# Rotating the queries of the last layer on VectorE across row groups, two tiles at once, in place of rotation matmuls

## What is computed

```python
def rope(t, pos):
    half = MLA_ROPE // 2          # 32
    ...
    t1 = t[..., :half].astype(jnp.float32)
    t2 = t[..., half:].astype(jnp.float32)
    return jnp.concatenate([t1 * cos - t2 * sin, t1 * sin + t2 * cos], axis=-1).astype(t.dtype)

q = (rms_norm_2(c_q, mla_q_norm_w) @ mla_w_uq).reshape(b_, l_, MLA_HEADS, MLA_NOPE + MLA_ROPE)
kv = (rms_norm_2(c_kv, mla_kv_norm_w) @ mla_w_ukv).reshape(b_, l_, MLA_HEADS, MLA_NOPE + MLA_V)
q_nope, q_rope = q[..., :MLA_NOPE], rope(q[..., MLA_NOPE:], positions)
```

## Time and profile before

| | us |
|---|---|
| median of three runs | 1755.0 (1753.88 to 1757.76) |
| profiled execution, device time | 1759.86 |
| its span, first to last instruction | 1758.1 |
| TensorE busy in matmuls | 1714.0 (97%) |
| VectorE busy | 1304.2 (74%) |
| ScalarE busy | 906.0 (52%) |
| GpSimd busy | 182.9 (10%) |
| mean granted TensorE clock | 0.990 |

### The profile page before, as it was taken

The page is one execution under the profiler, slowest core; times in us unless marked ns, Lnnn a source line. Parts: engine busy times, 40 slices in busy tenths (PEclk is TensorE's granted clock), DMA queues, the critical chain, the costliest instruction groups (busy, mean ns, idle before and its releaser), DMA issues.

```text
span 1758.1 us, 24063 instructions
## 1 busy us (share of the span) xinstructions
PE 1714.0 (97%) x9505; PEld 1471.9 (84%) x9505; DVE 1304.2 (74%) x1616; ACT 906.0 (52%) x1178; POOL 182.9 (10%) x200
## 2 busy tenths in 40 slices
PE   6899999999999999999999999999999999999997
PEld 5778888887888888888888888888888888888886
DVE  6889979786787766887677788966566667778654
ACT  6344443444465445665454667644444445566543
POOL 4321101011010110111010010001111000000001
PEclk9989999999999999999999999999999999999999
DMA  9989979774455566666677555666666565444563
GB/s 356 384 285 339 351 227 318 231 255 149 144 168 169 191 181 189 183 190 204 182 217 211 158 166 170 183 191 192 188 191 180 168 195 147 138 132 132 168 190 109
DMA packets 312288, 357.00 MB, mean 203 GB/s; under 512 B 11633, under 2 KB 285169, under 8 KB 312177
## 3 DMA queue, kind: packets, MB, share of 16 engines
q1 hardware_dynamic: 295792, 296.24, 55.9%
q0 software_dynamic: 16384, 59.22, 9.7%
HBM read 353.29 MB, written 2.13 MB: 202 GB/s over the span
## 4 chain that ended last, share of the span: by engine, by line
PE 70%; DVE 16%; ACT 6%; issue 4%; DMA 2%; POOL 1%; SPq 0%; DVEq 0%; ACTq 0%
PE psG L491 40%; PE psG L492 20%; DVE w_lo L421 6%; ACT w_hi L417 3%; DMA raw<-in_mem_w 2%; PE psG L485 2%; PE psG L487 2%; PE psG L486 2%; DVE ada_sum L1327 1%; DVE P L1275 1%; PE psH L1943 1%; DVE P L1280 1%; PE psH L1926 1%; DVE W L1830 0%; DVE gate_sum L1327 0%
## 5 line engine op out<-in xcount | busy, mean ns | idle before, releaser
L491 PE MATMUL psG<-xA,w_hi 128*128 128x512 f32 x2624 | 945.8, 404 | 1.2 <-DVE w_lo L421 0.6
L421 DVE TENSOR_TENSOR w_lo<-raw,w_hi 128x1024 fp32r<-128x1024 f32 (+1 forms) x560 | 697.2, 1258 | 209.2 <-ACT w_hi L417 207.5
L492 PE MATMUL psG<-xA,w_lo 128*128 128x256 f32 x2624 | 737.6, 281 | 0.0
L417 ACT ACTIVATE w_hi<-raw 128x1024 fp32r<-128x1024 f32 (+1 forms) x560 | 569.0, 1042 | 224.0 <-PE psG L492 164.8
L491 PEld LDWEIGHTS psG<-xA,w_hi 128*128 128x128 f32 x2624 | 494.9, 189 | 120.8 <-issue 4.7
L492 PEld LDWEIGHTS psG<-xA,w_lo 128*128 128x128 f32 x2624 | 497.8, 190 | 2.3 <-issue 1.4
L491 PE MATMUL psG<-yP,w_hi 128*128 128x512 f32 x960 | 337.3, 397 | 2.2 <-DVE yP L1888 1.0
L492 PE MATMUL psG<-yP,w_lo 128*128 128x256 f32 x960 | 267.8, 279 | 0.0
L491 PEld LDWEIGHTS psG<-yP,w_hi 128*128 128x128 f32 x960 | 180.2, 188 | 46.1 <-DVE yP L1888 1.3
L460 ACT ACTIVATE P<-psG 128x512 f32<-128x512 f32 (+2 forms) x103 | 60.8, 590 | 238.1 <-PE psG L492 238.1
L492 PEld LDWEIGHTS psG<-yP,w_lo 128*128 128x128 f32 x960 | 180.8, 188 | 0.0
(11 more groups left out here) (345 smaller groups left out, 1772.3 us busy)
## 6 DMA issues: line engine op xcount, KB each, us to landing
raw<-in_w_in SPq DMA_DIRECT2D x360, 512.0 KB, 3.8
raw<-in_w_out SPq DMA_DIRECT2D x128, 512.0 KB, 3.5
ada_ring<-in_w_ada POOLq DMA_DIRECT2D x96, 512.0 KB, 6.3
raw<-in_mem_w SPq DMA_DIRECT2D x32, 512.0 KB, 10.2
raw<-in_w_uq SPq DMA_DIRECT2D x24, 384.0 KB, 3.4
raw<-in_w_ukv SPq DMA_DIRECT2D x32, 128.0 KB, 2.5
raw<-in_w_ukv SPq DMA_DIRECT2D x16, 256.0 KB, 3.4
P<-in_memT SPq DMA_DIRECT2D x4, 512.0 KB, 7.2
```

The source lines that it names most:

```text
L417: nc.scalar.activation(high(n), low(n, raw), ACT.Copy).then_inc(hi_ready, 1)
L421: nc.vector.tensor_tensor(low(n), low(n, raw), high(n), ALU.subtract).then_inc(lo_ready, 1)
L491: nc.tensor.matmul(psG[:, bank + f, :], hi[:, w], x, start=first, stop=False)
L492: last = nc.tensor.matmul(psG[:, bank + f, S:2 * S], lo[:, w], x[:, 0:S], start=False, stop=end)
```

## The change

VectorE does the whole rotation, and does it for the two tiles of a unit together at place 3 of the G_UK half; place 3 of the G_UV half is empty. The product with cos goes over both tiles (128 rows, 512 columns). For the product with sin four instructions of 32 rows and 512 columns each read one group of 32 rows and write the neighbouring one. The sign that the rotation matrix carried is put into the table of sin once, in unit 0, by two instructions on rows 32 to 63 and 96 to 127. TensorE's rotation matmuls and the semaphore `rq_rot` are gone; `rq_done` counts to 4.

```diff
             def rope_hook(u, bb, p):
...
-                if p == 3:
-                    r = 2 * u + bb
-                    x = P[:, QT + 3 * r + 2, :]
-                    landed(dve, G_UQ, (3 * r + 2) // 2 + 1)
-                    dve.wait_ge(q["rq_rot"], r + 1)
-                    v.tensor_tensor(t_cos, x, cos, ALU.mult)
-                    link(v.tensor_tensor(t_sin, psH[:, BA, 0:S], sin, ALU.mult))
-                    v.tensor_tensor(x, t_cos, t_sin, ALU.add).then_inc(q["rq_done"], 1)
+                if bb == 0 and p == 3:
+                    if u == 0:
+                        for row in (32, 96):
+                            ins = v.tensor_scalar(sin[row:row + 32], sin[row:row + 32], -1.0, None, ALU.mult)
+                        link(ins)
+                    x = P[:, QT + 6 * u + 2:QT + 6 * u + 6:3, :]
+                    landed(dve, G_UQ, 3 * u + 3)
+                    v.tensor_tensor(x_cos, x, cos2, ALU.mult)
+                    for row in (0, 32, 64, 96):
+                        to, of = slice(row, row + 32), slice(row ^ 32, (row ^ 32) + 32)
+                        ins = v.tensor_tensor(x_sin[to], x[of], sin2[of], ALU.mult)
+                    link(ins)
+                    v.tensor_tensor(x, x_cos, x_sin, ALU.add).then_inc(q["rq_done"], 1)
...
-                if p == 2:
-                    r = 2 * u + bb
-                    if r:
-                        pe.wait_ge(q["rq_done"], r)
-                    else:
-                        pe.wait_ge(q["rk_done"], 1)
-                    landed(pe, G_UQ, (3 * r + 2) // 2 + 1)
-                    mm(psH[:, BA, 0:S], C("rot64"), P[:, QT + 3 * r + 2, :], start=True, stop=True)\
-                        .then_inc(q["rq_rot"], 1)
```

More of the change, by code:

```diff
@@ L241, in build @@
             "ma_s ma_mx ma_p ma_pn ma_t ma_pt ma_o ma_y sc_cv sc_tap sc_done f2_y f2_hi f2_lo "
-            "rp_red rp_tab rk_rot rk_done rq_rot rq_done cn_sq cn_pre cn_ss cn_rs cn_h cn_hi cn_lo "
+            "rp_red rp_tab rk_rot rk_done rq_done cn_sq cn_pre cn_ss cn_rs cn_h cn_hi cn_lo "
             "ml_s ml_mx ml_p ml_pn ml_t ml_pt ml_o ml_y zc_done m3_y m3_hi m3_lo f3_y f3_hi f3_lo fin_y gained last"
@@ L1789, in _ @@
             t_cos, t_sin = P[:, ROPE_T, :], P[:, ROPE_T + 1, :]
+            x_cos, x_sin = P[:, ROPE_T:ROPE_T + 2, :], P[:, ROPE_T + 2:ROPE_T + 4, :]
+            cos2, sin2 = (x.unsqueeze(1).broadcast_to([NP, 2, S]) for x in (cos, sin))
             dve.wait_ge(q["rp_tab"], 1)
@@ L1814, in _ @@
             dve.wait_ge(loaded["late"], 32)
-            dve.wait_ge(q["rq_done"], 8)
+            dve.wait_ge(q["rq_done"], 4)
             v.tensor_copy(W[64:128, 0:S], P[64:128, KR, :])
@@ L2192, in _ @@
                     run_products(pe, g, ukv_hook)
-            pe.wait_ge(q["rq_done"], 8)
+            pe.wait_ge(q["rq_done"], 4)
             pe.wait_ge(q["rk_done"], 2)
```

## The result

The changed kernel took 1772.5 us (median of 4 runs, 1769.0 to 1775.0), before 1755.7 alongside; ratio 1.0086, 95% interval 1.0066 to 1.0106. It is slower, by 16.8 us. The forecast was 1771.7 us, +16.7.

A forecast was written before the change was run, and what follows sets the result against it. VectorE's rotation of each unit's first tile, ahead of L1672 for which TensorE's L1926 waits, was taken to bound the stage. Order +11.1 and clock +5.6 gave +16.7 us: 1771.7 us against the median 1755.0, range 1763.5 to 1777.

The forecast's parts named there:

- TensorE has no slack at the turn: TensorE's turn of the probabilities (L1926) waits for VectorE's scaling (L1672); its idle time grows from 0.15 to 3.7 us.
- Short instructions cost like full ones: Each 32x512 product with sin on VectorE costs like a full 128x512, 688 ns; group 4.21 us in place of 1.13.
- Rival B: 32-row instructions on VectorE are cheap: group 2.16 us, +2.9 us in all, 1758 us, no change; chance 0.05.
- Changing rows costs the overlap: VectorE instructions on other rows than the one ahead do not overlap: 0.72 us per step in place of 0.60.
- Rival C: Moves between row groups on VectorE are slower, 0.5 us more per sin product: 8 us more, near 1780 us; chance 0.07.
- Eight rotation matmuls are worth 1.7 us, not 3.4: On TensorE only the four removed in the G_UV halves gain, 0.43 us each; those in the G_UK halves only lengthen waiting.
- Two sign flips +0.75 us, tail -0.3 us: VectorE's two sign flips in unit 0 add 0.75 us; without the last rotation, L1676 after unit 3 comes 0.3 us earlier.
- Order alone +11.1 us: Stage cost without the clock: 4 x (3.08 - 0.43) + 0.75 - 0.3 = +11.1 us.
- The fall of the clock +5.6 us: TensorE's clock falls from 2.4 to 1.2 GHz after each unit's wait: 1.4 us per unit, +5.6 us over four.
- two such stretches: Two four-microsecond stretches of slow TensorE clock, perhaps in one unit; a bound only, each stretch priced at 1.7 us.
- rival A: TensorE's clock stays at 1.00 through the waits: +9.0 to +11.1 us, 1764 to 1766 us; chance 0.28.
- the forecast's span: Kernel time with the fallen clock: 1768 us (overlapping price) to 1776 us (stalls at 1.7, unit 0 twice); chance 0.60.

The follow-up runs named there:

- e3: Changed kernel with the rotation behind the scaling of the probabilities on VectorE, not ahead of it: stage 58.3 us, kernel 1757.2 us, ratio 1.0003.
- e4: Kernel before, with its own one-tile rotation moved behind the scaling of the probabilities: stage 59.5 us, kernel 1755.9 us, ratio 0.9998.
- e2: Changed kernel with one 128x512 product with sin in place of the four of 32 rows, leaving out the swap of halves: stage 61.9 us.
- e7: Changed kernel rotating by rows, but one tile in each half of a unit, six instructions over 256 columns each time: stage 69.2 us.
- e8: Changed kernel with all four short products reading and writing rows 0 to 31, rotation not computed: group 3.72 us, stage 77.7 us.
- e6: Changed kernel with two tiles at a time, but rotated by one TensorE matmul per unit and one product with sin: stage 61.2 us.
- e5: e3 with VectorE's keys' tile preparation right behind the last rotation and TensorE's last-copy wait moved later: stage 56.0 us, kernel 1752.6 us, ratio 0.9977.
- e1: Changed kernel with 14 throwaway matmuls per unit filling TensorE's wait for the scaled probabilities: stage 70.7 us, kernel 1768.1 us, ratio 1.0076.

## Why the prediction was right

- *TensorE has no slack at the turn; what VectorE takes longer ahead of L1672, TensorE loses.* Right: the forecast wait of 3.7 us (4.4 in unit 0) measured 3.58 (4.27). e3 and e4 show it from the other side: with the rotation behind the scaling the wait is gone.
- *Short instructions cost like full ones.* Right. Forecast for the group 4.21 us, measured 4.11; e2 and e7 gave 1.93 and 2.52 us with other counts and lengths. Rival B is out.
- *Changing rows costs the overlap.* Right, with 0.70 us per step for 0.72; e8 takes it alone. Rival C, a dearer move between row groups, is out: all sixteen short products took 0.68 us.
- *Eight rotation matmuls are worth 1.7 us, not 3.4.* Not measured by itself, but the sums that rest on it came out within 0.1 us in e2 and e6. In e3 and e5, where TensorE does not wait at the turn, all eight leave its path, though part of that is lost again to the later copy L1676.
- *Two sign flips +0.75 us, tail -0.3 us.* Right. In unit 0 the reciprocal starts 6.00 us behind the L421 ahead of the group, in unit 1 5.25: 0.75 us. The idle time at the end of the stage went from 0.58 to 0.24 us.
- *Order alone +11.1 us.* The filled wait (e1) gave 70.7 - 60.0 = 10.7 us. The 0.4 us between them are the four groups, each 0.10 us shorter than forecast.
- *The fall of the clock +5.6 us.* It is 77.5 - 70.7 = 6.8 us. This is the one term that was sized too low, by 1.2 us. The 1.4 per unit held in units 1 to 3 (1.3 to 1.6 us); the miss is unit 0, with 2.4 us, where the clock stayed down for longer. The forecast had "two such stretches" in one unit only as a bound. For the same reason unit 0 is 19.4 us long, above the 16.5 to 18.6 forecast; the others, 18.34 and 18.65, are at its upper end. Why it is unit 0 stays open. That the fall comes in each unit, the part I was least sure of (rival A had 0.28), was right.
- *Two slips that change no forecast.* VectorE does have 0.25 us of free time between the add L1275 and L1672: L421 waits for ScalarE's high part, before as after, so the path goes through ScalarE there. And the upper end of the forecast's span is 1774.6 by its own terms (11.1 + 5 x 1.7 = 19.6), not 1776.

The two misses, -0.4 and +1.2 us, partly cancel: 17.4 us in the profiled stage, 16.7 forecast. That the medians differ by 16.8, within 0.1 us of the forecast, is luck: the interval of the ratio stands for +11.6 to +18.6 us.

## What to carry to other kernels

Ask of every instruction that is added to an engine which waiting instruction of another engine stands right behind it. Here 3 us more of VectorE work ahead of a 0.6 us scaling, in each of four units, cost 17 us, and the same work directly behind it, with the end of the stage put in order, made the kernel 0.2% faster, about half of it through the place and the end (an estimate). Read a wait from the starts of the instructions around it too: one listed as 0.15 us cost nearly 0.4. On VectorE count instructions and columns, not rows: a split into row groups multiplies the price, and changing rows each time takes away the overlap too. And when a stall on TensorE reaches a couple of microseconds, add the clock to its price: here it was 6.8 us on top of 10.7.

## What was not expected of the hardware

The length of a wait does not alone decide whether the clock falls. Waits of 1.97 to 1.98 us were followed by the half clock in three units of e7, the 2.67 us wait of unit 0 in the same execution was not, nor the 2.99 us wait near the start of the kernel, nor the 2.08 us wait of unit 0 in e2; the 2.37 us wait at the end of e3 was, and 3.19 and 3.58 us were in every unit. And what a fall costs varies within an execution (2.4 us in unit 0 of the changed kernel, 1.3 to 1.6 in the others) and between them: with shorter waits e8 had the longer slow time.
